# Query projection in quarters inside the attention steps, sample keys in strips of one head, and other seams between phases, in a hybrid decoder step

## What is computed

```python
for l in range(DEPTH):                      # DEPTH 2, N_A 1
    if l == N_A:
        kv = rms_norm(x, kv_norm) @ w_kv    # k rotated; shared keys and values
    x = x + 0.5 * swiglu_ffn(rms_norm(x, norm_ffn[l, 0]), ffn_w_in[l, 0], ffn_w_out[l, 0])
    h = rms_norm(x, norm_mix[l])
    if l < N_A:                             # pointwise, GLU, causal depthwise conv of width 31,
        mix, st = conv_module(h, ...)       # layer norm over channels, swish, pointwise
    else:
        q = rope((h @ w_q[j]).reshape(b, s, N_HEADS, 2, HEAD_DIM), pos)
        o = diff_attention(q, pos, k_all, v_all, k_pos, lam)   # softmax(1) - lam * softmax(2)
        o = rms_norm(o, subln_g[j]) * (1.0 - lam_init)
        mix = o.reshape(b, s, V_DIM) @ w_o[j]
    x = x + mix
    x = x + 0.5 * swiglu_ffn(rms_norm(x, norm_ffn[l, 1]), ffn_w_in[l, 1], ffn_w_out[l, 1])
return rms_norm(x, norm_final), ...
```

## Time and profile before

| | |
|---|---|
| median of 3 runs | 2153.24 us (2152.76 to 2153.68) |
| profiled execution | 2152.26 us, span 2150.4 us |
| mean granted clock of TensorE | 0.974 |
| busy: PE, DVE, ACT, POOL | 2047.5, 937.4, 671.8, 485.2 us |

### The profile page before, as it was taken

One profiled execution on the slowest core, in us unless ns is written; L12 is line 12 of the kernel. 1 busy time (PEld: TensorE's weight loads), 2 busy tenths in 40 slices (PEclk: granted clock), 3 DMA queues, 4 the chain that ended last, 5 costly groups with the idle time before them and its releaser, 6 DMA issues.

```text
span 2150.4 us, 39532 instructions
## 1 busy us (share of the span) xinstructions
PE 2047.5 (95%) x16188; PEld 1967.6 (91%) x16188; DVE 937.4 (44%) x1124; ACT 671.8 (31%) x1041; POOL 485.2 (23%) x323
## 2 busy tenths in 40 slices
PE   7999999999799999999999999999767799999997
PEld 7999999988499999999999999999744599999996
DVE  4444333599653333333533333333577343333322
ACT  5222222444542222222132222222244442222221
POOL 1223311022123233110402332111411122233210
PEclk9999999999899999999999999999968899999998
DMA  5333332266233333332643333323544233323331
GB/s 181 97 89 88 104 103 82 74 133 127 43 89 90 97 88 89 109 93 82 177 114 94 88 89 98 109 86 118 160 157 164 77 91 97 89 88 98 102 94 40
DMA packets 355196, 219.67 MB, mean 102 GB/s; under 512 B 7700, under 2 KB 339861, under 8 KB 354973
## 3 DMA queue, kind: packets, MB, share of 16 engines
q1 hardware_dynamic: 339188, 192.29, 30.4%
q0 software_dynamic: 6000, 14.47, 3.3%
q10 hardware_dynamic: 9928, 11.79, 1.8%
HBM read 198.52 MB, written 7.53 MB: 96 GB/s over the span
## 4 chain that ended last, share of the span: by engine, by line
PE 91%; DVE 3%; DMA 2%; ACT 2%; issue 1%; POOL 0%; SPq 0%; ACTq 0%; DVEq 0%; POOLq 0%
PE ps_all L525 85%; PE ps_all L547 2%; PE ps_all L626 1%; PE ps_all L602 1%; PE ps_all L534 1%; PE ps_all L674 1%; DVE s_dec L1390 1%; DVE kprod L1387 1%; DMA vT<-v_new_out 1%; DMA raw<-w_in 0%; DMA made<-made 0%; PE ps_all L615 0%; PE ps_all L579 0%; ACT t_act L919 0%; PE ps_all L636 0%
## 5 line engine op out<-in xcount | busy, mean ns | idle before, releaser
L784 ACT ACTIVATE w_hi<-raw 128x1024 fp32r<-128x1024 f32 (+1 forms) x296 | 334.6, 1130 | 1263.7 <-PE ps_all L525 1256.9
L525 PE MATMUL ps_all<-xg_hi,w_hi 128*128 128x260 f32 x3456 | 701.4, 284 | 15.5 <-DVE xg_lo L1065 11.6
L525 PE MATMUL ps_all<-xg_hi,w_lo 128*128 128x260 f32 x3456 | 698.5, 284 | 0.0
L525 PE MATMUL ps_all<-xg_lo,w_hi 128*128 128x260 f32 x3456 | 697.7, 284 | 0.0
L525 PEld LDWEIGHTS ps_all<-xg_hi,w_hi 128*128 128x128 f32 x3456 | 536.1, 189 | 17.4 <-DVE w_lo L1055 14.3
L525 PEld LDWEIGHTS ps_all<-xg_hi,w_lo 128*128 128x128 f32 x3456 | 535.1, 189 | 0.0
L525 PEld LDWEIGHTS ps_all<-xg_lo,w_hi 128*128 128x128 f32 x3456 | 533.8, 189 | 0.0
L1055 DVE TENSOR_TENSOR w_lo<-raw,w_hi 128x1024 fp32r<-128x1024 f32 (+1 forms) x296 | 397.3, 1342 | 268.0 <-ACT w_hi L784 268.0
L525 PE MATMUL ps_all<-h_hi,w_hi 128*128 128x260 f32 x1664 | 341.3, 285 | 9.3 <-DVE h_lo L1248 9.3
L525 PE MATMUL ps_all<-h_hi,w_lo 128*128 128x260 f32 x1664 | 338.9, 283 | 0.0
L525 PE MATMUL ps_all<-h_lo,w_hi 128*128 128x260 f32 x1664 | 338.3, 283 | 0.0
(11 more groups left out here) (158 smaller groups left out, 1108.2 us busy)
## 6 DMA issues: line engine op xcount, KB each, us to landing
raw<-w_in SPq DMA_DIRECT2D x176, 512.0 KB, 3.7
raw<-w_out SPq DMA_DIRECT2D x64, 704.0 KB, 4.5
raw<-c_in SPq DMA_DIRECT2D x16, 512.0 KB, 3.9
raw<-w_kv SPq DMA_DIRECT2D x16, 512.0 KB, 4.0
page<-cache_k SPq DMA_DIRECT2D x16, 512.0 KB, 3.7
page<-cache_v SPq DMA_DIRECT2D x16, 512.0 KB, 4.4
made<-made POOLq DMA_DIRECT2D x28, 256.0 KB, 4.6
t_out<-t_gate ACTq DMA_DIRECT2D x64, 65.0 KB, 2.1
```

What stands on the lines that cost most here:

```text
L525: mm = nc.tensor.matmul(unit[slot][:, s, :], w[:, c % 2, k * P:(k + 1) * P], m[:, s * HALF:(s + 1) * HALF], start=kk == 0 and i == 0, stop ...
L784: nc.scalar.activation(w_hi[:, c % 2, 0:w], raw[:, c, 0:w], ACT.Copy).then_inc(hi_made, 1)
```

## The change

- Start: the first weight chunk is loaded and rounded in halves, squares and sums go between the inputs, the parts of the third chunk come before the norm, the lambda sum after it.
- conv_in: taps 18, 6, 7 in place of 19, 7, 5, and 16, 11, 4 for the last tile; another tree of accumulating DMAs, seven per tile; of the norm's squares three are summed on DVE; conv_out opens with two chunks interleaved (`ramp`).
- v: the inputs of up2 are made during the last v chunk; the last transposition stands inside up2's first chunk.
- q: three chunks whole, the other five in four pieces each (`piece`: 12 matmuls into PSUM bank 5) in steps 0 to 19. Scores of steps 0 and 1 stand inside the third chunk.
- Samples: keys in 16 strips of one head and four samples (eight DMAs each, `K_AT` names their steps); the queries go through `q_dram` per head (`pass_q`); values in halves of a page with matmuls of one column (`V_AT`), with no transpositions after them.
- End: the last sum of squares goes into the matmul group.

```diff
-DVE_TAPS, PE_TAPS, ACT_TAPS = 19, 7, 5
-LAST_TAPS = (19, 12)
+DVE_TAPS, PE_TAPS, ACT_TAPS = 18, 6, 7
+LAST_TAPS = (16, 11, 4)
+BATCH = NS // 2
+Q_FIRST, Q_SLOTS = 3, 3
...
-        V_AT = {17: 0, 19: 1, 21: 2, 23: 3, 25: 4, 27: 5, 29: 6, 31: 7}
+        SCORES_AT = (12, 28)
+        TURN_AT = (14, 30)
+        V_AT = {23: (0, 0), 24: (0, 2), 25: (0, 4), 26: (0, 6), 32: (1, 0), 33: (1, 2), 34: (1, 4), 35: (1, 6)}
+        K_AT = {s: i for i, s in enumerate((1, 2, 3, 4, 5, 6, 8, 10, 12, 14, 16, 18, 20, 22, 24, 25))}
...
+            def load_k(i, page_ids):
+
+                h, j = divmod(i, 2)
+                if i >= 2:
+                    sp.wait_ge(kprod_done, i - 1)
+                for g in range(NPG):
+                    for b in range(BATCH):
+                        pg = page_ids[NPG * (BATCH * j + b) + g]
+                        strip = cache_k[bass.ds(pg, 1), :, h * P:(h + 1) * P].rearrange("a t f -> (a t) f")
+                        sp.dma_start(k_strips[:, i % 2, BATCH * g + b, :], strip).then_inc(k_full[i % 2], 16)
+
+            def pass_q(h):
+
+                sp.wait_ge(q_s_made, h + 1)
+                sp.dma_start(q_dram[h].rearrange("(b f) -> f b", b=NS), q_s[:, h, :],
+                             allow_slow_non_contiguous=True).then_inc(q_stored, 16)
+                sp.wait_ge(q_stored, 16 * (h + 1))
+                if h:
+                    sp.wait_ge(kprod_done, 2 * h)
+                sp.dma_start(qb[:, :, :].rearrange("p b f -> p (b f)"), q_dram[h:h + 1, :].broadcast_to([P, NS * P])
+                             ).then_inc(qb_full, 16)
+
+            def load_v(n, i, page_ids):
+
+                if n:
+                    sp.wait_ge(v_page_used, i // NPG + 1)
+                strip = cache_v[bass.ds(page_ids[i], 1), :, n * SEQ:(n + 1) * SEQ].rearrange("a t f -> (a t) f")
+                sp.dma_start(v_pages[:, i, :], strip).then_inc(v_page_full[i], 16)
...
+                for h in range(HEADS):
+                    pass_q(h)
+                    if h == 6:
+                        sp.wait_ge(chunk_used, ph.chunk0 + ph.chunks)
+                        for i in range(NS * NPG):
+                            load_v(0, i, page_ids)
+                    if h + 1 < HEADS:
+                        load_k(2 * h + 2, page_ids)
+                        if h in (0, 2, 3, 4):
+                            load_chunk(o, 0, (0, 2, 3, 4).index(h))
+                        if h in (5, 6):
+                            load_chunk(o, 1, h - 5)
+                        load_k(2 * h + 3, page_ids)
+                for i in range(NS * NPG):
+                    load_v(1, i, page_ids)
+                load_chunk(o, 1, 2)
+                load_chunk(o, 1, 3)
...
+            def last_variance(sums):
+
+                pe.wait_ge(rstd_made, made)
+                pe.wait_ge(summed, sums - 1)
+                mean(0, acc[:, :], ps_stat)
+                pe.wait_ge(squared, SQUARES_BEFORE["down", 3] + KD)
+                mean(KD - 1, sq[:, 1, :], ps_stat).then_inc(var_done, 1)
...
+            def piece(s):
+
+                ph, (k, i) = KIND["q"][0], divmod(s, 4)
+                m = Q_FIRST + k
+                if i == 0:
+                    pe.wait_ge(drained, Q0 + m)
+                if i == 2:
+                    pe.wait_ge(half_drained, k + 1)
+                half = KD // 2
+                chunk(ph, m // 4, m % 4, tiles=range(i % 2 * half, (i % 2 + 1) * half), halves=(i // 2,), to=q_bank)
 
...
+            def sample_values(n, b):
+
+                pe.wait_ge(d_turned_read, n + 1)
+                if n == 0 and b == 0:
+                    pe.wait_ge(drained, Q0 + KD)
                 for g in range(NPG):
-                    pe.wait_ge(v_page_full[NPG * b + g], 16)
-                for g in range(NPG):
-                    for c in range(2):
-                        mm = nc.tensor.matmul(ps_all[c * HD:(c + 1) * HD, 5, :], at_dec[g][:, b * HD:(b + 1) * HD],
-                                              V_ALL[v_slot(NPG * b + g)[0]][:, c * SEQ:(c + 1) * SEQ],
-                                              start=b == 0 and g == 0, stop=b == NS - 1 and g == NPG - 1)
-                mm.then_inc(v_page_used, NPG)
+                    pe.wait_ge(v_page_full[NPG * b + g], 16 * (n + 1))
+                for h in range(BATCH):
+                    at = n * HD // 2 + h * NS + b
+                    for g in range(NPG):
+                        mm = nc.tensor.matmul(ps_all[:, 5, at:at + 1], v_pages[:, NPG * b + g, h * P:(h + 1) * P],
+                                              at_dec[:, g, at:at + 1], start=g == 0, stop=g == NPG - 1)
...
+                def ramp():
+
+                    half = KD // 2
+                    chunk(ph, 0, 0, tiles=range(half))
+                    for k in range(half):
+                        chunk(ph, 0, 1, tiles=range(k, k + 1))
+                        chunk(ph, 0, 0, tiles=range(half + k, half + k + 1))
+                    chunk(ph, 0, 1, tiles=range(half, KD))
...
+                        if 4 * g + c == KD - 1:
+                            for m in range(KD):
+                                if m < KD - 1:
+                                    act.wait_ge(xg_free, m + 1)
+                                else:
+                                    act.wait_ge(chunk_used, ph.chunk0 + ph.chunks)
+                                x_hi(4, m)
                         ahead(ph, g, c)
...
+                dve.wait_ge(four_added, 16 * KD)
+                dve.wait_ge(joined, KD)
+                nc.vector.tensor_tensor(a, a, products[1][0], ALU.add).then_inc(joined, 1)
+                dve.wait_ge(joined, KD + 1)
                 finish(KD - 1, (KD - 1) % 2)
 
...
+                def strip_scores(i):
+
+                    h, j = divmod(i, 2)
+                    dve.wait_ge(k_full[i % 2], 16 * NPG * BATCH * (h + 1))
+                    if j == 0:
+                        dve.wait_ge(qb_full, 16 * (h + 1))
+                    q = qb[:, BATCH * j:BATCH * (j + 1), :].unsqueeze(1).broadcast_to([P, NPG, BATCH, P])
+                    strips = k_strips[:, i % 2, :, :].rearrange("p (g b) f -> p g b f", g=NPG)
+                    nc.vector.tensor_tensor(kprod[:, :, :].rearrange("p (g b) f -> p g b f", g=NPG), strips, q, ALU.mult
+                                            ).then_inc(kprod_done, 1)
+                    dve.wait_ge(kprod_done, i + 1)
+                    nc.vector.tensor_reduce(s_dec[:, :, h, BATCH * 2 * j:BATCH * 2 * (j + 1)],
+                                            kprod[:, :, :].rearrange("p (g b) (c d) -> p g (b c) d", g=NPG, c=2), AX.X, ALU.add
+                                            ).then_inc(kred_done, 1)
 
...
+                def into_conv(m):
+                    pool.wait_ge(seven_added, 16 * (m + 1))
+                    pool.wait_ge(conv_done, m + 1)
+                    pool.dma_start(conv[:, m, 0:SEQ], products[m % 2][0], accum_op=ALU.add).then_inc(conv_added, 16)
+
+                for m in range(KD):
+                    p, pairs = products[m % 2], shares(m)[2] // 2
+                    for i in range(pairs):
+                        pool.wait_ge(products_made, ACT_TAPS * m + 2 * i + 2)
+                        pool.dma_start(p[2 * i], p[2 * i + 1], accum_op=ALU.add).then_inc(pair_added[i], 16)
+                    if m:
+                        into_conv(m - 1)
+                    pool.wait_ge(pair_added[0], 16 * (m + 1))
+                    pool.wait_ge(pair_added[1], 16 * (m + 1))
+                    pool.dma_start(p[0], p[2], accum_op=ALU.add).then_inc(four_added, 16)
+                    if m == KD - 1:
+                        continue
...
-                    pool.dma_start(conv[:, m, 0:SEQ], p[:, 0, :], accum_op=ALU.add).then_inc(conv_added, 16)
+                    pool.wait_ge(pair_added[2], 16 * (m + 1))
+                    pool.dma_start(p[4], p[6], accum_op=ALU.add).then_inc(three_added, 16)
+                    pool.wait_ge(four_added, 16 * (m + 1))
+                    pool.wait_ge(three_added, 16 * (m + 1))
+                    pool.dma_start(p[0], p[4], accum_op=ALU.add).then_inc(seven_added, 16)
```

545 lines of the change are left out of this document (291 added, 254 removed).

## The result

The changed kernel took 2241.65 us (median of 4 runs, 2239.86 to 2242.45) against 2153.1 us for the kernel before: ratio 1.041, 95% interval 1.0392 to 1.0428. The forecast of 2142 and its range of 2120 to 2168 are both missed, on the slower side. The profiled execution has a span of 2240.5 us, 90.1 more than before, and the chain has moved.

The account below looks back on a forecast made before the run. TensorE's weight-chunk matmuls were taken to bound most of the span, with VectorE also full in conv_in and busier in the attention. Terms -2.2-12.3-4.5-0.7+8.7=-11.0 gave 2141.3, 2142 as a median; range 2120 to 2168.

Parts of the forecast that it names:

- the queries' round trip: Attention: each head's queries go to memory and back; price C = 11.2 us from issues, write, read and semaphores.
- rival C: Attention: the round trip is long and the kernel slower, 2174 at C=15.2, breaking even at C=12.6; chance 0.25.
- now 27.0, as two of them hold half the value products: Late attention: the 7 steps after step 24's arrival take 27.0 us, where 7 steps took 25.1 before.
- the tail's 14.9: After the last at_n: 64 one-column value products at 0.233 each, 14.9 us; half clock could add up to 15.
- On this count alone the attention would gain: Attention: VectorE's work per head falls from 20.4 to 18.2 us, a gain before pricing the round trip.
- The start, -2.2,: Kernel start: earlier w_lo, no lambda wait before it and interleaved squares save 2.2 us, between 0.5 and 3.
- conv_in, -9.7 to the centring,: conv_in and its tail: fewer taps on VectorE and TensorE let centring start at 552.2 in place of 561.92.
- Rival D: conv_in does not gain: more accumulating DMAs make ScalarE wait, 8 to 12 of the 12.3 lost; chance 0.13.
- The 0.9 for the squares: Layer norm after conv_in: three squares summed on VectorE in place of 12 more TensorE matmuls give 0.9 us.
- 1.7 for its opening: conv_out's opening: two interleaved chunks give TensorE work while tiles are made, 1.7 us gained (0 to 3).
- The v seam, -4.5,: After v's last chunk: inputs made earlier and the last transposition inside the next chunk give 1114.2 in place of 1118.7.
- the end, -0.7,: Kernel end: VectorE's last sum of squares leaves the chain as TensorE takes both parts, saving 0.7 us.

Follow-up runs that it names:

- The probes: Eight writes to scratch memory in different piece patterns, added in SyncE's queue ahead of the k phase to e3_old_attention, each waited for: 1.4 to 10.7 us.
- e6_wide: Changed kernel with queries written in 32-byte runs, plus value products of 64 equal columns in place of one: 2166.38 us, ratio 1.0062.
- e10_no_trip: Changed kernel with 64-column value products, only head 0's sample queries written and read, once, and used for every head's strips: 2143.36 us, ratio 0.9962.
- e3_old_attention: Kernel before with the changes of the start, conv_in, the v seam and the end; q and attention as before: 2129.28 us, ratio 0.9893.
- e9_early_wide: Changed kernel with queries in 32-byte runs, written ahead of the odd strip's loads, and 64-column value products: 2159.16 us, ratio 1.0031.

## Why the prediction was wrong

**The step that failed** is "the queries' round trip", C = 3.2 + 4.0 + 3.7 + 0.3 = 11.2, "between 9.0 and 15.2". Issues were 3.9 and the read 4.0, near enough; the write was 11.4, outside its bounds of 2.1 and 6.6. I said that no row shows such pieces, and then bounded them by 31 ns a packet, a mean over weight loads in runs of 512 bytes and more, as if a piece cost a share of an engine's time. The probes show that it doesn't: the engines idle, and the place in memory makes the difference of 2.6 and 10.5 for the same pieces. Of the 79.5 us missed up to head 7's first strip, the eight writes account for 57 (89.4 in place of 32) and the issues for 6 (eight of 3.9 in place of 3.2). The other 16 were not told apart; they lie in the steps, whose work ran at granted clocks of 0.65 to 0.76. The mechanism was the one named as rival C, with its break-even of C=12.6, and only its size was out of range: C=15.2, +4.0 a trip, gave 2174; the real 19.6 is 8.4 a trip, +67.

**A second step was mis-sized**, "now 27.0, as two of them hold half the value products", and the tail's 14.9. From head 7's first product to the last combination it was 38.7 us in place of 27.0, and from there to the statistics 31.6 in place of 19.8. 64 products in steps 23 to 26 and 64 behind cost 52.0 us of TensorE, 0.43 each for most; at full clock a product takes 3.68/16=0.23, exactly the price I used. The prediction named the half clock as able to cost 15 more, and had no reason to expect it; the reason is in the products' single column, as `e6_wide` shows. And I let half of them cost 1.9 us, in the belief that VectorE paces those steps. `e10_no_trip` has no round trip to wait for there and products at nearly the full price of 0.23, and its stretch is still 17.4 us longer than the old one, at a granted clock of 0.90 in 1650 to 1700: VectorE waited 15.1 us for TensorE's scores in it, and 8.2 in the old one, with a block of products of 3.7 to 4.2 us in TensorE's queue in each of four steps. That points to TensorE as what paces those steps.

**"On this count alone the attention would gain"** was wrong too, by the same run: without the round trips step 24 is level with the old attention (0.7 us), not before it. The 18.2 us a head, in place of 20.4, is VectorE's work alone; from step 8 to step 24 a head took 22.4 there. In 1470 to 1700 VectorE waited 27.5 us for TensorE's scores and 26.0 for ScalarE's `h_hi`, which the sum put at nothing. Which of them set the period was not tried.

**The start, -2.2,** was -5.6 in the trace and -4.5 by itself. Two terms were missing: TensorE opens 1.9 us earlier (8.32 in place of 10.24), since half a weight chunk is enough, and the stretch of 30 to 40 us ran at 0.71 before, behind the wait of 3.86, and at 1.00 now. The 60 records of that window became 85.

**conv_in, -9.7 to the centring,** was -9.4, by its own steps: the glu period fell from 17.94 to 17.28 us, 0.66. Rival D had the DMA share right (0.87 in 440 to 530, from 0.67) and the consequence wrong; accumulating DMAs rose from 4.6 to 5.8 us and stayed hidden. The 0.9 for the squares was 0.3 at the full clock; in the changed kernel the 20 records ran at 0.70 and cost 1.9 more than in `e3_old_attention` (6.82 and 4.97). From conv_out's first product to the seam the gain was 2.7 (528.2 us, from 579.37 to 1107.55, and 525.5, from 565.93 to 1091.39) where I had 1.7 for its opening.

**The v seam, -4.5,** was -4.5 and **the end, -0.7,** was -1.1. One slip of adding changes nothing: 1692.3 and 19.8 make 1712.1, not 1711.9.

## What to carry to other kernels

A DMA that scatters single elements has to be timed by itself before it is put on a chain, in the very pattern it will have: 128 of them side by side cost as much as 1024, and 64 bytes between them took three quarters of the time away. A round trip through memory that begins only when the work behind it is done is paid whole, once per repetition; issue its first half as early as its data is there. Matmuls of one column cost 0.43 us each here at a granted clock of 0.50, and 0.23 with the column repeated 64 times, so repeat it, or put the small operand on the stationary side; and a change of several parts should be run part by part, since here the four around the attention gained 23 us by themselves and the attention lost 112.

## What the runs showed that I had not expected

- A store of 128 pieces of 4 bytes to neighbouring addresses took 9.9 us, one of 1024 such pieces 10.5 and 10.7, one of 1024 pieces 64 bytes apart 2.6, and one of 128 runs of 32 bytes 1.4.
- TensorE, busy 42.69 of 43 us with matmuls of one column, had a granted clock of 0.50; with 64 columns a product, 16 of them took 3.68 us in place of 6.83, at the same number of weight loads; only the first such block, behind steps at 0.50, still took 6.93 in `e9_early_wide`.
- A VectorE product whose second operand is read at a stride of 32 bytes took 2.07 us for 128x1024 in place of 1.25.
- Behind a wait of 3.86 us at the start TensorE's clock stood at 0.71 for the next 10 us; with 1.56 of waiting it stayed at 1.00.
